# The second layer of a two-layer block as one interleaved program by token halves

## What is computed

```python
for layer in range(DEPTH_2):                     # 2
    if layer % 2 == 0:
        ...
        tok = causal_attention(q, k, v).reshape(b, s, TOK_WIDTH)          # 12 heads
    else:
        z = h @ lru_w_in[j]
        u, gate, q_mem = _split(z, [TOK_WIDTH, MIX_WIDTH, MEM_WIDTH])     # 768, 1024, 256
        tok = rg_lru_branch(u, ...)
    mem_kv = (mem @ w_mem_kv[layer]).reshape(b, MEM_LEN, 2, N_MEM_HEADS, HEAD_DIM)
    mem_out = memory_attention(q_mem..., mem_kv[:, :, 0], mem_kv[:, :, 1])  # 4 heads, 256 keys
    y = jnp.concatenate([tok, mem_out], axis=-1) * jax.nn.silu(gate)
    h = layer_norm(ALPHA * h + y @ w_out[layer], ln_g[layer], ln_b[layer])

def rg_lru_branch(...):
    xc = conv_b + sum of four causal taps of u
    r, i = sigmoid(xc @ w_r + b_r), sigmoid(xc @ w_i + b_i)   # blocks of 64
    a = exp(log_a), log_a = c * r
    hs = scan of a * hs + sqrt(1 - a * a) * (i * xc)
```

## Time and profile before

| | us |
|---|---|
| median of 3 runs | 3805.05 |
| lowest, highest | 3798.99, 3806.5 |
| the profiled execution, its time | 3795.12 |
| its span, first to last instruction | 3793.4 |
| end of the first attention, in the span | 3003.4 |

### The profile page before, as it was taken

One profiled execution on the slowest core, in us unless ns is written; L12 is line 12 of the kernel. 1 busy time (PEld: TensorE's weight loads), 2 busy tenths in 40 slices (PEclk: granted clock), 3 DMA queues, 4 the chain that ended last, 5 costly groups with the idle time before them and its releaser, 6 DMA issues. The chain is left out here.

```text
span 3793.4 us, 46895 instructions
## 1 busy us (share of the span) xinstructions
PE 3326.3 (88%) x17764; PEld 2603.0 (69%) x17764; DVE 1937.3 (51%) x2828; ACT 1121.1 (30%) x2218; POOL 1382.9 (36%) x1115
## 2 busy tenths in 40 slices
PE   6898999998899998899999999998799897942776
PEld 3776787886788886677888788776565565821463
DVE  3287854455455555867335533742288524157434
ACT  4145431333333333312111111222366403123213
POOL 1115644643344321666666666655200110000020
PEclk9988879999899999999999999999899998975588
DMA  4345444321444423433333333353422102310121
GB/s 157 101 132 143 147 133 154 91 81 50 132 122 120 111 73 99 145 91 89 100 95 95 95 95 99 88 150 104 136 57 70 41 19 67 94 54 11 48 68 45
DMA packets 500295, 360.56 MB, mean 95 GB/s; under 512 B 93057, under 2 KB 449270, under 8 KB 500086
## 3 DMA queue, kind: packets, MB, share of 16 engines
q1 hardware_dynamic: 487126, 318.93, 29.1%
q0 software_dynamic: 6912, 25.17, 2.1%
q10 hardware_dynamic: 6048, 13.63, 1.0%
HBM read 269.51 MB, written 87.62 MB: 94 GB/s over the span
## 5 line engine op out<-in xcount | busy, mean ns | idle before, releaser
L3014 PE MATMUL psum<-place,place 128*128 128x512 f32 x1614 | 647.0, 401 | 61.6 <-POOL place L2991 34.4
L3015 PE MATMUL psum<-place,place 128*128 128x512 f32 x1614 | 634.0, 393 | 0.0
L3016 PE MATMUL psum<-place,place 128*128 128x512 f32 x1614 | 633.7, 393 | 0.0
L2991 POOL TENSOR_TENSOR place<-place,place 128x1024 fp32r<-128x1024 f32 (+3 forms) x238 | 521.6, 2191 | 19.0
L2989 POOL CAST place<-place 128x1024 fp32r<-128x1024 f32 (+3 forms) x238 | 229.6, 965 | 540.9 <-PE psum L3016 364.9
L3014 PEld LDWEIGHTS psum<-place,place 128*128 128x128 f32 x1614 | 306.4, 190 | 151.0 <-POOL place L2991 46.2
L3015 PEld LDWEIGHTS psum<-place,place 128*128 128x128 f32 x1614 | 306.6, 190 | 66.4 <-issue 4.6
L3016 PEld LDWEIGHTS psum<-place,place 128*128 128x128 f32 x1614 | 306.1, 190 | 65.1
L659 PE MATMUL psum<-place,place 128*128 128x512 f32 (+1 forms) x712 | 289.2, 406 | 20.7 <-issue 10.4
L661 PE MATMUL psum<-place,place 128*128 128x512 f32 (+1 forms) x712 | 274.1, 385 | 0.0
L660 PE MATMUL psum<-place,place 128*128 128x512 f32 (+1 forms) x712 | 273.8, 385 | 0.0
(11 more groups left out here) (340 smaller groups left out, 6335.8 us busy)
## 6 DMA issues: line engine op xcount, KB each, us to landing
place<-in_w_mlp_up SPq DMA_DIRECT2D x64, 512.0 KB, 4.0
place<-in_w_mlp_down SPq DMA_DIRECT2D x64, 512.0 KB, 3.8
chunked<-place SPq DMA_DIRECT2D x64, 320.0 KB, 3.6
place<-in_w_in SPq DMA_DIRECT2D x34, 512.0 KB, 5.7
...
```

Of the source, the lines that this page charges most:

```text
L2991: nc.gpsimd.tensor_tensor(lo, raw, hi.bitcast(F32), ALU.subtract).then_inc(self.w_split, 1)
L3014: pe.matmul(ps, self.w_hi[:, j, k, :], hi, start=(k == 0), stop=False)
L3015: pe.matmul(ps, self.w_hi[:, j, k, :], lo, start=False, stop=False)
L3016: mm = pe.matmul(ps, self.w_lo[:, j, k, :], hi, start=False, stop=(k == kt - 1))
```

## The change

Ten stages behind `trunk` become one, `rest`. h, u, gates and queries of layer 1 stay on chip; nothing goes to DRAM between the first attention and the output. The projections are 64 tiles of one `Chain`, each for 512 tokens: 16 of `w_out_2[0]`, 32 of `lru_w_in_2`, 16 of `w_out_2[1]`, the first half of the tokens ahead of the second in each. `Chain` gets two kinds: `alpha` adds ALPHA times h on DVE and sums the rows for the mean, `silu_to` makes x times sigmoid(x) in place. `LayerNorms` is in seven steps beside tiles, with one fp32 product for the mean and one for the variance. `Lru` takes the root of 1 - a * a as (1 + a²) times tanh, with a square on ACT and no reciprocal; it has nine rounds of three steps. `Recall` is the memory attention of layer 1 as an `Attend` on what lies on chip, with one PSUM bank for transposes and one for values. `TurnOut` transposes from h without a copy. `rest` writes the order by hand. `mixer` now puts one memory pair first and one last, and its queues run straight on into the tiles: SP's weight loads stand behind its last loads. The functions `turn_in`, `turn_out`, `norm`, `linears`, `attention`, `memory_attention`, `move`, `silu_gate` and `lru` go. In the lists, tile numbers count from the first tile of `rest`: 0 to 15, 16 to 47 (L is 16), 48 to 63 (W1 is 48).

```diff
+            elif kind == "alpha":
+                x = t["x"]
+                dve.wait_ge(self.done, n + 1)
+                stt(x, x, ALPHA, ps, ALU.mult, ALU.add).then_inc(self.evac[j], 1)
+                if t["nth"]:
+                    if t["nth"] > 1:
+                        dve.wait_ge(self.totalled, t["total"])
+                    dve.wait_ge(self.evac[j], n // 2 + 1)
+                    tt(t["into"], t["prev"] if t["nth"] == 1 else t["into"], x, ALU.add).then_inc(self.totalled, 1)
+            elif kind == "silu_to":
+                dve.wait_ge(self.opened, t["gated"] + 1)
+                tt(t["dst"], ps, t["dst"], ALU.mult).then_inc(self.evac[j], 1)
...
+class LayerNorms:
...
+    def tensor(self, pe):
+        ones = self.C.mat("ones")
+        for i, m in enumerate(self.units):
+            pe.wait_ge(self.chain.totalled, (KD - 1) * (i + 1))
+            if i:
+                pe.wait_ge(self.mean, i)
+                pe.wait_ge(self.root, i)
+            pe.matmul(self.mean_ps, ones, m["acc"], start=True, stop=True).then_inc(self.total, 1)
+            for _ in range(3):
+                yield
+            pe.wait_ge(self.added, (KD - 1) * (i + 1))
+            pe.matmul(self.var_ps, ones, m["rstd"], start=True, stop=True).then_inc(self.var, 1)
+            for _ in range(self.slots - 3):
+                yield
...
+            dve.wait_ge(self.total, i + 1)
+            self.C.nc.vector.tensor_scalar(m["acc"], self.mean_ps, 1.0 / D, None, ALU.mult).then_inc(self.mean, 1)
+            dve.wait_ge(self.mean, i + 1)
+            for k in range(KD // 2):
+                centre(k)
+            yield
+            for k in range(KD // 2, KD):
+                centre(k)
+                add(k - KD // 2 + 1)
+            yield
+            for k in range(KD // 2 + 1, KD):
+                add(k)
+            yield
+            yield
+            dve.wait_ge(self.root, i + 1)
+            self.C.nc.vector.reciprocal(m["rstd"], m["rstd"]).then_inc(self.rec, 1)
+            dve.wait_ge(self.rec, i + 1)
+            for k in range(KD // 2):
+                scale(k)
+            yield
+            for k in range(KD // 2, KD):
+                scale(k)
+                low(k - KD // 2)
+            yield
+            for k in range(KD // 2, KD):
+                low(k)
+            yield
...
+class Lru:
...
+    def tensor(self, pe):
+        C = self.C
+        for i in range(self.NT + 3):
+            t = i - 1
+            if 0 <= t < self.NT:
+                if t == 0:
+                    pe.wait_ge(self.b_ready, 64)
+                pe.wait_ge(self.conv, 3 * t + 3)
+            for x in range(2):
+                if 0 <= t < self.NT:
+                    if 2 * t + x:
+                        pe.wait_ge(self.sig, 2 * t + x)
+                    for c in range(2):
+                        mm = pe.matmul(C.psum[:, 2 + c, :], self.blocks[:, x, t, :],
+                                       self.xc[:, t % 2, 512 * c:512 * c + 512], start=True, stop=True)
+                    mm.then_inc(self.prod, 1)
+                yield
+            yield
...
+    def scalar(self, act):
+        nc, C, NT = self.C.nc, self.C, self.NT
+        for i in range(NT + 3):
+            t = i - 2
+            if 0 <= t < NT:
+                act.wait_ge(self.sq, t + 1)
+                r = self.R[:, t % 2]
+                nc.scalar.activation(r, r, ACT.Sqrt, scale=-1.0, bias=C.cols[:, 50:51]).then_inc(self.root, 1)
+            t = i - 3
+            if 0 <= t:
+                act.wait_ge(self.gated, t + 1)
+                nc.scalar.activation(self.hi[:, t, :], self.R[:, t % 2], ACT.Copy).then_inc(self.y_hi, 1)
+            t = i
+            if t < NT:
+                self.landed(act, self.u_tile(t))
+                if t == 0:
+                    act.wait_ge(self.dpre, self.PRE)
+                if t >= 2:
+                    act.wait_ge(self.gx, t - 1)
+                nc.scalar.activation(self.xc[:, t % 2], self.u[:, t, :], ACT.Identity, scale=C.par("lru_conv", 18 + t),
+                                     bias=C.par("lru_conv_b", t)).then_inc(self.tapped, 1)
+            yield
+            t = i - 1
+            if 0 <= t < NT:
+                b = t % 2
+                if t >= 2:
+                    act.wait_ge(self.ready, t - 1)
+                for x, (dst, bias) in enumerate(((self.R, "lru_b_r"), (self.Ig, "lru_b_i"))):
+                    act.wait_ge(self.prod, 2 * t + x + 1)
+                    nc.scalar.activation(dst[:, b], C.psum[:, 2:4, :].rearrange("p a b -> p (a b)"), ACT.Sigmoid,
+                                         bias=C.par(bias, t)).then_inc(self.sig, 1)
+                act.wait_ge(self.sig, 2 * t + 2)
+                nc.scalar.activation(self.av[:, b], self.R[:, b], ACT.Exp, scale=self.lam[:, t:t + 1])\
+                    .then_inc(self.exped, 1)
+                act.wait_ge(self.exped, 3 * t + 1)
+                nc.scalar.activation(self.R[:, b], self.R[:, b], ACT.Tanh, scale=self.lam[:, t:t + 1])\
+                    .then_inc(self.exped, 1)
+                nc.scalar.activation(self.u[:, t, :], self.av[:, b], ACT.Square).then_inc(self.exped, 1)
+            yield
+            yield
...
+    def vector(self, dve):
+        nc, C, NT = self.C.nc, self.C, self.NT
+        tt, stt = nc.vector.tensor_tensor, nc.vector.scalar_tensor_tensor
+        for i in range(NT + 3):
+            t = i - 3
+            if 0 <= t:
+                dve.wait_ge(self.y_hi, t + 1)
+                tt(self.lo[:, t, :], self.R[:, t % 2], self.hi[:, t, :].bitcast(F32), ALU.subtract)\
+                    .then_inc(self.ready, 1)
+            t = i
+            if t < NT:
+                x = self.xc[:, t % 2]
+                dve.wait_ge(self.tapped, t + 1)
+                for d in range(1, 4):
+                    if d > 1:
+                        dve.wait_ge(self.conv, 3 * t + d - 1)
+                    stt(x[:, d:T], self.u[:, t, 0:T - d], C.par("lru_conv", 6 * (3 - d) + t), x[:, d:T], ALU.mult,
+                        ALU.add).then_inc(self.conv, 1)
+            yield
+            t = i - 1
+            if 0 <= t < NT:
+                b = t % 2
+                dve.wait_ge(self.sig, 2 * t + 2)
+                tt(self.Ig[:, b], self.Ig[:, b], self.xc[:, b], ALU.mult).then_inc(self.gx, 1)
+            t = i - 2
+            if 0 <= t < NT:
+                b = t % 2
+                dve.wait_ge(self.root, t + 1)
+                dve.wait_ge(self.gx, t + 1)
+                tt(self.Ig[:, b], self.Ig[:, b], self.R[:, b], ALU.mult).then_inc(self.scaled, 1)
+            t = i - 1
+            if 0 <= t < NT:
+                b = t % 2
+                dve.wait_ge(self.exped, 3 * t + 3)
+                stt(self.R[:, b], self.u[:, t, :], 1.0, self.R[:, b], ALU.add, ALU.mult).then_inc(self.sq, 1)
+            yield
+            t = i - 2
+            if 0 <= t < NT:
+                b = t % 2
+                dve.wait_ge(self.scaled, t + 1)
+                nc.vector.tensor_tensor_scan(self.R[:, b], self.av[:, b], self.Ig[:, b], 0.0, ALU.mult, ALU.add)\
+                    .then_inc(self.scanned, 1)
+                for n in self.gate_tile(t):
+                    self.landed(dve, n)
+                dve.wait_ge(self.scanned, t + 1)
+                tt(self.R[:, b], self.R[:, b], self.gate[:, t, :], ALU.mult).then_inc(self.gated, 1)
+            yield
...
+class Recall(Attend):
+    DEPTH = PV = 1
...
+class TurnOut:
...
+    def tensor(self, pe):
+        C = self.C
+        for t in range(T // P):
+            pe.wait_ge(self.norm.shifted, KD * (3 + t // 4))
+            if t >= 2:
+                pe.wait_ge(self.copied, 2 * t - 2)
+            for q in range(2):
+                for k in range(4):
+                    mm = pe.transpose(C.psum[:, 4 + 2 * (t % 2) + q, k * P:(k + 1) * P],
+                                      self.x[:, 4 * q + k, P * t:P * t + P], C.mat("ident"))
+                mm.then_inc(self.turned, 1)
+            yield
+    def scalar(self, act):
+        for t in range(T // P):
+            if t >= 2:
+                act.wait_ge(self.stored[t % 2], 16 * (t // 2))
+            for q in range(2):
+                act.wait_ge(self.turned, 2 * t + q + 1)
+                self.C.nc.scalar.activation(self.nat[:, t % 2, 512 * q:512 * q + 512],
+                                            self.C.psum[:, 4 + 2 * (t % 2) + q, :], ACT.Copy).then_inc(self.copied, 1)
+            yield
...
+def rest(C, h, q96, kn, krope, v2, gate, qm, km, vm, out):
...
+    def output(l):
+        for s in range(SEG):
+            hi, lo = operand(y_hi, y_lo, s)
+            for t in range(KD):
+                tiles.append(dict(src=cols(ins["w_out_2"][l, :, :], t), kt=KD, hi=hi, lo=lo, kind="alpha", nth=t,
+                                  x=h[:, t, seg(s)], prev=h[:, max(t - 1, 0), seg(s)], into=small[s], s=s))
...
```

(58 more changed lines are left out.)

1100 lines of the change are left out of this document (325 added, 775 removed).

## The result

| | before | after |
|---|---|---|
| median, us | 3802.02 (4 runs beside those of after) | 3629.56 (4 runs) |
| lowest, highest | 3783.88, 3806.5 | 3608.29, 3637.11 |
| the profiled execution, its time | 3795.12 | 3632.03 |
| its span | 3793.4 | 3630.2 |

The ratio is 0.9546, 95% interval 0.9494 to 0.9598: faster by 4.5%. The prediction was 3527 us with a range of 3486 to 3598. The direction was right, the size was not: the profiled execution gained 163.2 us of the 278.1 foretold, and 114.9 are missing.

What follows compares the result with a forecast made beforehand. The part after the first attention was taken as bound stage by stage by different engines, each working alone. Its 790.0 us become 516.3, less 4.4 at the head: a gain of 278.1 from 3805.05, so 3527 us, range 3486 to 3598.

Steps and rivals of the forecast that it cites:

- What bounds the kernel: The 790.0 us after the first attention: bound stage by stage by different engines, each working alone.
- The 64 tiles: Projections after the first attention: 5.42 us a tile, 346.7 us in all; loading and splitting weights twice costs nothing.
- Layer norms: Norms beside tiles: PE pays 3.6 us for six fp32 products; DVE's some 36 of 38 us just fits, no charge.
- Memory attention, first half: 16 steps between tiles 26 and 31, 1.36 us each plus table loads: 30 us added, bounds 22 and 45.
- LRU: Nine rounds beside tiles 37 to 45, 17.2 us for a round: 63 us added, bounds 35 and 88.
- Memory attention, second half: Last 19 steps after tiles 46 and 47, uncovered: 30 us, bounds 26 and 56, plus 5 for low-clock restarts.
- Tail: After tile 63: uncovered last norm 25.4 us, four turned blocks 11.2, closing 0.4; 37 us, bounds 32 and 45.
- Head: First attention's start, memory pair first: 4.4 us less wait for loads, bounds 0 and 7; its other order changes nothing.
- A: Clock stays low from tile 38 until the last projection, not only at restarts: 45 us more, 3572; chance 0.24.
- B: ScalarE's table switches cost double, 1.28 us more on each of 20: 26 us more, 3553; chance 0.06.
- C: Engines overlap better in the LRU's rounds and the first memory steps: 36 us less, 3491; chance 0.14.
- D: POOL's split, slowed by DVE's traffic, paces all tiles; 10.2 us a split would give 3830 us; chance 0.02.

Runs made afterwards that it cites:

- e2: Against the changed kernel, GpSimd splits only one of eight row blocks of each weight tile from the second layer's third tile on; 3579.92 us.
- e5: Against the changed kernel, the second layer's norms read mean and reciprocal root from PSUM, and three of four write their squares there; 3594.40 us.
- e3: Changed kernel with the second memory attention's steps spread, one or two behind a weight tile, instead of in two groups; 3621.76 us.
- e1: Changed kernel with the first attention's six latent pairs first and the memory pairs last, as in the kernel before; 3640.86 us.
- e6: As e1, but GpSimd begins to split the second layer's weights only when the first attention's last block is evicted; 3626.08 us.
- e4: Changed kernel with the LRU's second gate product in two further PSUM banks; the memory attention's second half waits for the LRU's last sigmoid; 3591.74 us.

## Why the prediction was right or wrong, by its steps

*What bounds the kernel* was right: three stages with one engine each were laid over each other, and their waits are gone.

By terms of the sum the 114.9 us are: 39.2 at the tiles beside norms, 23.6 at the LRU (tiles 38 to 45: 130.0 us, 106.4 given), 10.4 and 9.6 at the memory steps, 14.8 at the first attention, 5.6 at the tail, 9.7 in the trunk, 2 elsewhere. The norms beside tiles and the order of the first attention had been given no charge and no bounds, so even the sum of all high ends, 3605 us, lies under the measured 3630.

*The 64 tiles.* The pace of 5.42 us stands wherever nothing disturbs it, and POOL's split (1.15 + 2.69 = 3.8 us in the mean from 3020 us on) ended no wait of PE there. "That costs nothing" was the failed step. The question was put only as: is POOL fast enough? The price lay on the other side, in what POOL does to DVE. The Trainium skill's rule that GpSimd contends with VectorE instructions of two SBUF inputs ("GPSIMD Engine Reference", Key points) was weighed for POOL's slowing alone. The runs agree with the rule itself (1271 to 684 ns in e2, and 680 in e5 with one operand in PSUM), and they show the direction that mattered here. The trace of before held the number, and I didn't read it. Groups of DVE in the norm of the trunk there, 2400 to 2700 us, beside the splits:

```profile
L3172 DVE SCALAR_TENSOR_TENSOR place<-place,params,place 128x512 f32<-128x512 f32 x18 | 23.1, 1315 | 0.0
L3106 DVE TENSOR_TENSOR solve<-psum,solve 128x512 f32<-128x512 f32 x16 | 11.0, 688 | 46.0 <-ACT solve L3074 46.0
```

*Layer norms.* "This just fits; no charge" failed by 27.5 and 11.7 us. The passes were priced at 0.7 us from a norm that had stood alone; beside POOL they took 0.96 to 1.27. With 36 of 38 us claimed there was no room for even a tenth more. The prediction had named this as what would make it wrong. A reading failed too: the 64 that took 31.0 us in the earlier trace rows are instructions, and a product is two of them. A tile with a norm's product in it takes 6.3 us in place of 5.4, so the six cost about 5.4 us, not 3.6.

*Memory attention, first half.* 39.6 us over the tiles where 29.6 stood (its terms add up to 29.4), inside the bounds of 22 and 45. A step alone behind a tile cost 1.7 in e3; in groups the waits behind the table loads and the low clock come on top.

*LRU.* The loop was found and its order was right; the term was mis-sized. The round came out at 21.75 us and not 17.2, past the 4 us that were named. Against the loop's 16.1 us: 2.8 us are the second gate product, counted as two instructions of 0.5 where there are four of 0.47 at full clock (twice that after a pause), 2.9 are scan and gating beside POOL.

*Memory attention, second half.* 45.4 us over its tiles, and 30 + 5 were given: the price of a step nearly held (1.48 in the group of 13, 2.1 at the low clock in the group of 6), the 12.1 us for the exp behind the LRU were missing. With the splits cut down (e2) that wait was 3.9.

*Tail.* The norm is as predicted (3587.6 to 3613.5 us, 25.9, for 25.4). The last four turned blocks take 16.7 us, where 11.2 and 0.4 were given. Half of the old time was the wrong measure: 32 transposes after a pause of 8.64 us, at the low clock, take 6.16 us, and the first 32 of the kernel before took 6.06 just so (3773.03 us, after 13.12); that start and the last store are paid once, for four blocks as for eight.

*Head.* 4.0 us gained, 4.4 foretold. But "the rest of its order changes nothing" failed by 14.8 us: e1 and e6 show that the order decides at which clock the first 50 us run. The other order waits 7 to 8 us longer for its first loads, so of the 14.8 us it would have won back little.

*Rivals.* A (the clock stays low) came half true: 0.78 over tiles 38 to 45 and 0.79 over 46 and 47, coming back to 1.00 within 3.4 us of the start of the next tile each time. B is refuted: a pass starts 1.29 us after its table load began (3372.68, 3373.97). The Trainium skill ("ScalarE: Activation LUTs", What ACT_TABLE_LOAD costs) has about 2.66 us for a switch; these rows do not show it. C's rounds of 13 us need e4, whose rounds take 9 to 20. D did not come: from 3015 us on no wait of PE was ended by POOL. And 9.7 us of the missing gain are the trunk's own variation.
